# Early heads' one-hot tables of places made by GpSimd and ScalarE instead of VectorE

## What is computed

```
q = (hb @ w_q).reshape(C, PEER_HEADS, 2, PEER_DK_HALF)
s = jnp.einsum('thpd,hpnd->thpn', q, sub_keys).astype(jnp.float32)
sv, si = lax.top_k(s, PEER_TOPK)
cand = sv[:, :, 0, :, None] + sv[:, :, 1, None, :]
cidx = si[:, :, 0, :, None] * PEER_NKEYS + si[:, :, 1, None, :]
...
fv, fpos = lax.top_k(cand, PEER_TOPK)
eidx = jnp.take_along_axis(cidx, fpos, axis=-1).reshape(C, PEER_HEADS * PEER_TOPK)
g = jax.nn.softmax(fv, axis=-1).reshape(C, PEER_HEADS * PEER_TOPK)
```

## Time and profile before

| | us |
|---|---|
| median of 3 runs | 2003.02 |
| lowest, highest | 2001.21, 2003.94 |
| profiled execution, its own time | 2005.09 |
| its span | 2003.3 |
| TensorE busy | 1960.2 (98%) |
| VectorE, ScalarE, GpSimd busy | 1366.8, 792.7, 858.7 |
| mean granted TensorE clock of the span | 0.997 |

### The profile page before, as it was taken

One profiled execution on the slowest core, in us unless ns is written; L12 is line 12 of the kernel. 1 busy time (PEld: TensorE's weight loads), 2 busy tenths in 40 slices (PEclk: granted clock), 3 DMA queues, 4 the chain that ended last, 5 costly groups with the idle time before them and its releaser, 6 DMA issues.

```text
span 2003.3 us, 27875 instructions
## 1 busy us (share of the span) xinstructions
PE 1960.2 (98%) x9978; PEld 1440.4 (72%) x9978; DVE 1366.8 (68%) x3012; ACT 792.7 (40%) x1815; POOL 858.7 (43%) x680
## 2 busy tenths in 40 slices
PE   9999999999999999999999999999999999999998
PEld 8888876888768875788876666666666666666564
DVE  6742034333374566649999988888888888877767
ACT  3222233123563327621271575555556455410100
POOL 3544432428444753424424454443444434343343
PEclk9999999999999999999999999999999999999999
DMA  7655642515202411134489999999999999999999
GB/s 284 211 185 180 162 114 106 190 63 168 94 1 59 126 35 54 43 126 137 129 322 370 421 415 422 421 421 422 409 420 421 415 421 416 410 421 417 412 423 300
DMA packets 93644, 529.27 MB, mean 264 GB/s; under 512 B 10160, under 2 KB 14688, under 8 KB 44000
## 3 DMA queue, kind: packets, MB, share of 16 engines
q1 hardware_dynamic: 50112, 248.73, 33.5%
q0 software_dynamic: 37728, 270.55, 33.2%
q10 hardware_dynamic: 5696, 8.66, 2.1%
HBM read 520.56 MB, written 7.34 MB: 264 GB/s over the span
## 4 chain that ended last, share of the span: by engine, by line
DMA 26%; PE 22%; DVE 16%; POOL 4%; issue 2%; ACT 1%; another core or an unknown queue 0%; DVEq 0%; POOLq 0%; ACTq 0%
DMA work<-in_peer_uv,consts 14%; DMA ring<-in_peer_uv,consts 13%; PE ps L887 9%; PE ps L1325 3%; PE ps L1300 3%; DVE tables L2221 2%; POOL ring L2932 2%; DVE work L2196 1%; POOL work L2932 1%; DVE ring L2196 1%; PE ps L1192 1%; PE ps L937 1%; DVE work L1979 1%; DVE ring L2178 1%; DVE work L1972 1%
## 5 line engine op out<-in xcount | busy, mean ns | idle before, releaser
L1325 PE MATMUL ps<-work,tmp 128*128 128x512 f32 x1008 | 448.8, 598 | 16.0 <-DVE tmp L2255 15.9
L1300 PE MATMUL ps<-hT,work 128*128 128x256 f32 x1984 | 449.4, 381 | 0.0
L1300 PEld LDWEIGHTS ps<-hT,work 128*128 128x128 f32 x1984 | 373.3, 190 | 75.4 <-issue 29.7
L2832 POOL TENSOR_TENSOR w_lo<-ring,w_hi 128x1024 fp32r<-128x1024 f32 (+2 forms) x112 | 267.1, 2390 | 333.2 <-ACT w_hi L2337 314.6
L1325 PEld LDWEIGHTS ps<-work,tmp 128*128 128x128 f32 x1008 | 190.5, 191 | 240.4 <-issue 213.2
L2932 POOL DMA_INDIRECT ring<-in_peer_uv,consts x128 | 206.6, 1614 | 289.0 <-DVE tables L2221 255.2
L2932 POOL DMA_INDIRECT work<-in_peer_uv,consts x128 | 204.6, 1598 | 281.9 <-DVE tables L2221 224.7
L2337 ACT ACTIVATE w_hi<-ring 128x1024 fp32r<-128x1024 f32 (+2 forms) x116 | 120.4, 1041 | 359.9 <-PE ps L887 320.8
L2694 ACT ACTIVATE ring<-iota,consts 128x128 f16<-128x128 f32 x768 | 231.5, 426 | 0.0
L2196 DVE CUSTOM_DVE_ANT_0 ring<-ring,tables 128x1024 f32<-128x1024 f32 x128 | 155.7, 1222 | 70.6 <-DMA ring<-in_peer_uv,consts 68.4
L2747 ACT ACTIVATE hT<-hT 128x4 f32<-128x4 f32 (+1 forms) x66 | 13.6, 206 | 479.6 <-DVE hT L2196 479.5
(11 more groups left out here) (392 smaller groups left out, 3153.7 us busy)
## 6 DMA issues: line engine op xcount, KB each, us to landing
work<-in_peer_v SPq DMA_DIRECT2D x64, 1024.0 KB
work<-in_u_steps SPq DMA_DIRECT2D x62, 1024.0 KB
ring<-in_a_w_in SPq DMA_DIRECT2D x48, 512.0 KB, 4.3
ring<-in_ada_w SPq DMA_DIRECT2D x48, 512.0 KB, 5.0
ring<-in_peer_w_q SPq DMA_DIRECT2D x32, 512.0 KB, 3.5
ring<-in_a_w_out SPq DMA_DIRECT2D x16, 512.0 KB, 4.1
ring<-in_b_w_in SPq DMA_DIRECT2D x16, 512.0 KB, 4.3
ring<-in_c_in SPq DMA_DIRECT2D x12, 512.0 KB, 3.9
```

Source lines behind the costliest of these rows:

```text
L1300: mm = pe.matmul(ps[:, 4 + s, j * DT:(j + 1) * DT], u[s][:, j, k, :], hT[:, k, GATHERED * P:T], start=(k == 0), stop=(k == KD - 1))
L1325: mm = pe.matmul(ps[:, 2 * t + half, :], tmp[:, s, j * DT + t * P:j * DT + (t + 1) * P], v_ring[:, s, j, half * BANK:(half + 1) * BANK], s ...
L2832: pool.tensor_tensor(w_lo[q % NPIECE][:, 0:n], ring[:, at:at + n], w_hi[q % NPIECE][:, 0:n], ALU.subtract).then_inc(w_split, 1)
```

## The change

For heads 0 to 6 the two tables are made in three steps elsewhere. GpSimd, once `placed` tells it that `posf` is there, subtracts the counter from it (`place_off`). ScalarE squares the difference in place and then takes max(0, 1 - square) in place, so that 0 becomes 1 and every other whole number becomes 0 (`place_hot`). GpSimd waits for that and goes on as before. ScalarE does this in a function `hot_places`, which stands in its queue at seven fixed turns, `HOT_AT`: turns 0 to 16 are the early queries, turn 17 + f is late query f. So heads 0 to 4 are served right behind the copies of early queries 5, 8, 11, 13 and 15, heads 5 and 6 behind those of late queries 2 and 4. Head 7 stays with VectorE, with a new wait for the picks of head 5. To have semaphores for this, the four of the slabs of `x` become one, and ScalarE waits for all four slabs ahead of the first square. GpSimd also waits once for the load of `iota`.

```diff
+HOT_AT = (5, 8, 11, 13, 15, 19, 21)
...
-                for a in range(2):
-                    one_hot_place(step, r, NE, a, pick_eq[h % 2][a])
+                if h == PEER_H - 1:
+                    dve.wait_ge(picked, 2 * (h - 1))
+                    for a in range(2):
+                        one_hot_place(step, r, NE, a, pick_eq[h % 2][a])
...
+                    act.wait_ge(x_loaded, 16 * NT)
                     for t in range(NT):
-                        act.wait_ge(x_loaded[t], 16)
...
+            def hot_places(turn):
+
+                for h in range(PEER_H - 1):
+                    if HOT_AT[h] != turn:
+                        continue
+                    for a in range(2):
+                        eq = pick_eq[h % 2][a]
+                        act.wait_ge(place_off, 2 * h + a + 1)
+                        act.activation(eq, eq, ACT.Square).then_inc(place_hot, 1)
+                        act.wait_ge(place_hot, 4 * h + 2 * a + 1)
+                        act.activation(eq, eq, ACT.Relu, scale=-1.0, bias=1.0).then_inc(place_hot, 1)
+
             for f in range(2 * PEER_H + 1):
                 if f < 2 * PEER_H:
                     keep_query("pqT", "peer_s", f)
+                hot_places(f)
...
                     keep_late(f - 1)
+                hot_places(2 * PEER_H + 1 + f)
...
+            pool.wait_ge(row_loaded, 16 * 7)
             for h in range(PEER_H):
...
                 pool.wait_ge(placed, h + 1)
+                if h < PEER_H - 1:
+                    if h >= 2:
+                        pool.wait_ge(picked, 2 * (h - 1))
+                    for a in range(2):
+                        pool.tensor_tensor(pick_eq[h % 2][a],
+                                           early[h % 2].posf[:, a, :].unsqueeze(2).to_broadcast([P, EK, TOPK]),
+                                           iota[:, 0:TOPK].unsqueeze(1).to_broadcast([P, EK, TOPK]),
+                                           ALU.subtract).then_inc(place_off, 1)
                 for a in halves:
+                    if h < PEER_H - 1:
+                        pool.wait_ge(place_hot, 4 * h + 2 * a + 2)
```

More of the change, by code:

```diff
@@ L587, in network @@
         x_again = sem("x_again")
-        x_loaded = [sem(f"x_loaded{t}") for t in range(NT)]
+        x_loaded = sem("x_loaded")
         xT_loaded = [sem(f"xT_loaded{q}") for q in range(KD // 2)]
@@ L654, in network @@
         placed = sem("placed")
+        place_off = sem("place_off")
+        place_hot = sem("place_hot")
         pick_step = sem("pick_step")
@@ L764, in _ @@
                     for t in range(NT):
-                        sp.dma_start(a_x[:, t, :], ins["x"][t * P:(t + 1) * P, :]).then_inc(x_loaded[t], 16)
+                        sp.dma_start(a_x[:, t, :], ins["x"][t * P:(t + 1) * P, :]).then_inc(x_loaded, 16)
                     sp.dma_start(ident[:], ins["ident"]).then_inc(const_loaded, 16)
```

## The result

The changed kernel has a median of 2007.01 us (14 runs, 2004.59 to 2008.10) against 2003.71 us for the kernel before in the same comparison (14 runs). The ratio is 1.0015, 95% interval 1.0008 to 1.0022: some 3 us slower, 1.6 to 4.4. Two later comparisons gave 1.0009 (1.0000 to 1.0018) and 1.0013 (1.0004 to 1.0022). All three point the same way: it is slower. All three also lie within 0.2% in the middle, so it is the class that was forecast, no change beyond 0.2%; the size, 2.0 to 3.3 us between the medians, is larger than the forecast's 1.0.

What follows compares the result with a forecast made beforehand. TensorE and VectorE, both full, were taken to meet balanced at the tables `pairs`. 0 from VectorE and +0.8 us of TensorE's wait, +1.0 with larger activations half weighed, on 2003.02 gave 2004.0 us, range 2000.0 to 2009.0.

Steps and rivals of the forecast that it cites:

- the meeting point: At tables `pairs`, about 1000 us: TensorE and VectorE both full, VectorE at most about 0.1 us late; faster VectorE gains 0.
- the wait of TensorE: Near 961 us, for ScalarE's copy of late query 0 behind head 4's tables: 0.8 us, range 0.3 to 1.5.
- the forecast's own signs: Heads 2 to 4 waiting for GpSimd, head 7 near 986.5, VectorE idle 4 to 5 us, tables 1000.6 to 1001.8 us.
- A sign of being wrong: In VectorE's routing heads: above 11.3 us a head without a wait in them would speak for slower heads.
- the forecast's own 2001.2 to 2006.3: For the whole kernel: from no TensorE wait and no stall to a 1.5 us wait and the 1.8 us stall doubled.
- the slower rival: VectorE's heads lengthen with GpSimd busy beside them: 2007.1 us at 11.8 us a head, 2013 at 12.8; chance 0.13.
- a head's 10.26 us: VectorE's routing heads without two tables: 11.56 - 1.30, about 10.26 us each; 9.1 us gross gain over seven heads.
- second rival: VectorE's short instructions wait for GpSimd's, an estimated 2.4 us a head, a pace of 12.7 us; chance 0.13.
- threshold of 11.8 us: VectorE's head length giving TensorE waits of 2.4 us near 961 and 1.7 us at turn 21: +4.1 us, 2007.1.
- The rule of the Trainium skill: In VectorE's heads: two-SBUF-input instructions and GpSimd's SBUF reads exclude each other, conversions possibly too; line 1993 showed 0.1 us.
- The sum: Whole kernel: 0 from VectorE, +0.8 us from TensorE's wait, +1.0 us with larger activations half weighed; median 2004.0 us.
- the fourth rival: VectorE and ScalarE's unnamed 1.8 us stall at 1024.43 us can vanish or double: 1.8 us either way; no separate chance.

Runs made afterwards that it cites:

- experiment 5: Kernel before with one semaphore for the slabs of x, plus two more 128x512 GpSimd operations a head in heads 0 to 6; ratio 1.0029 (1.0018 to 1.0040).
- experiment 3: Kernel before without VectorE's tables of heads 0 to 6, GpSimd multiplying a zero in their place; ratio 1.0005 (0.9996 to 1.0015).
- the turns moved: Changed kernel with HOT_AT (5, 8, 11, 14, 17, 20, 23) instead of (5, 8, 11, 13, 15, 19, 21); ratios to the kernel before 1.0007 and 1.0001.
- experiment 2: Kernel before with only one semaphore and one wait for the four slabs of x; ratio 1.0002 (0.9993 to 1.0011).
- four activations: Kernel before with one semaphore for x; ScalarE waits for head 4's `placed` at turn 15 and makes four 128x512 activations; 2007.82 us, ratio 1.0008.
- six activations: Kernel before with one semaphore for x; ScalarE waits for head 4's `placed` at turn 15 and makes six 128x512 activations; ratio 1.0019 (1.0010 to 1.0028).
- experiment 4: Eleven late queries ahead of `pairs` instead of twelve: in the kernel without VectorE's tables of heads 0 to 6, ratio 1.0000; in the kernel before, 1.0030.

## Why the prediction was right, and where it was off

**What luck did.** The class came out as forecast, because the meeting point gives nothing back and the wait of TensorE is small. But most of the forecast's own signs did not come: heads 2 to 4 did not start on a wait for GpSimd, head 7 was placed at 991.08 and not near 986.5, VectorE did not idle 4 to 5 us, and the tables came at 1002.43, behind 1001.8. A sign of being wrong did come: heads of about 11.3 us and more without a wait in them. The 2007.01 us lie outside the forecast's own 2001.2 to 2006.3, in the part of the range that was there for the slower rival (the kernel before measured 0.7 us more this time than in the three runs). And it was luck that the contention took no more than the tables gave back: VectorE came to the tables 1.0 us early instead of 4.9, and experiment 5 shows what a late one costs.

**Right, and shown.** (a) The meeting point at `pairs` is balanced, and a faster VectorE is worth nothing there: experiment 3. (b) The change costs one wait of TensorE, for late query 0, because ScalarE stands at turn 15 for head 4: present in all three profiles, gone with the turns moved together with the 2.6 us. (c) An activation of 128x512 takes 0.61 to 0.63 us, against 0.6 taken. (d) The slabs of `x` cost nothing: experiment 2. (e) The first indirect transfer shows the shift: 2.12 us, as the tables (2.15).

**The step that failed: a head's 10.26 us.** I took VectorE's pace without the tables as 11.56 - 1.30 and let ScalarE's turns hold heads 2 to 4 by waits for the picks. Heads 0 to 6 came 11.0 to 12.3 us apart, 11.5 in the mean, and no head started on a wait for GpSimd. Experiment 3 shows 10.2 us where GpSimd has no more to do than before, so the subtraction was right for VectorE alone; experiment 5 shows what was missing, two operations of GpSimd for 0.7 us a head of VectorE, where the changed kernel lost 1.2. My second rival had the mechanism and about its size: it gave 11.3 us a head as the case where the sum still counts as no change, with a wait of 1.9 us near 961. A wait of 1.51 to 1.90 us came, and its threshold of 11.8 us wasn't reached. What the forecast had against it, that VectorE's heads stayed at 11.56 us with GpSimd beside them half the time, was a wrong reading: GpSimd's work lay beside the searches, which it doesn't slow. Only three short instructions grew, and the earlier trace rows had shown one of them at 276 instead of 195 ns.

The rule of the Trainium skill that the prediction named (SBUF — State Buffer, section "Who interferes with whom") fits these runs in kind: the adds with two inputs grew by up to 1.13 us (0.41 to 1.54) and the conversion by up to 1.1 (0.195 to 1.30), less than the 1.27 us of the operation of GpSimd beside them, and the searches not at all.

**From there the other sizes.** Head 7 was placed at 991.08 and not at 986.5, and VectorE idled 1.0 us ahead of `pairs` and 1.4 us ahead of the third table, not 4 to 5. Head 4 was placed 1.5 us later than forecast; the differences took 1.05 us each, not 1.27, so ScalarE began at 957.03 instead of 955.8. The block from there to the copy of late query 0 took 5.5 us, 0.3 less than forecast, so the copy was 0.9 us later than forecast and TensorE's scores behind it 1.7 us later than before (0.8 + 0.9), 1.51 us of that as a wait of its own; the scores behind the wait and turn 21 added 0.3 us. The sum with it would have been +2.0 us, a time of 2005.0; measured were 2.0 to 3.3 us, 0.4 of them outside the span.

**Left open: the 1.8 us of the earlier trace rows near 1024 us.** VectorE and ScalarE wait there, and each can only wait for one count of TensorE, `spread_summed`, which TensorE raises behind the 32 matmuls of a step (line 1291). In the kernel before the matmuls that VectorE's step needs end at 1024.10 us by their rows, and both engines go on at 1026.25, 2.1 us behind. In other profiles VectorE goes on 0.03 to 0.05 us behind such an end. First the kernel before, then the one with four activations, where the end is at 1025.87:

```profile
1026.25 0.42 DVE L2173 TENSOR_TENSOR ysum<-xres,consts 128x512 f16<-128x512 f16 x1 [1.82 <-remote]
```

```profile
1027.24 0.42 DVE L2174 TENSOR_TENSOR ysum<-xres,consts 128x512 f16<-128x512 f16 x1 [1.05 <-PE ps L1292]
```

Of the thirteen profiles, the five with all three tables at their old place have the full stall. In seven where a table has moved the count is not 2.1 us late: 1.2 and 1.4 in two (two more operations on GpSimd, four activations), and no idle time of that kind in the rest. But the thirteenth, the third profile of the changed kernel, has it in full with the tables moved. How much of a shift is left at the dense products goes with the stall. Tables 2.0 us late and no stall: 2.0 - 1.8 = 0.2, measured 0.3 to 0.4. Tables 1.8 late and 1.05 us of the stall left: 1.0, measured 1.0. Tables 4.8 late and no stall (six activations): 3.0, measured 3.3. Tables 2.4 late and nearly the whole stall: 2.3, measured 2.1. This is the fourth rival's 1.8 us, either way. Why the count comes late, no profile says; I didn't find an edit that would separate it.

**Left open: the way from there to the end.** The first two profiles of the changed kernel have the dense products only 0.3 to 0.4 us late, yet all three comparisons have it 2.0 to 3.3 us slower. The last dense product starts 1068.7, 1069.1 and 1069.8 us behind head 0 in the changed kernel, 1068.3 and 1068.0 with the turns moved; but the kernel before and its twin with one semaphore are themselves 1.2 us apart there (1066.4 and 1065.2). One profile a kernel can't trace the rest. The first indirect transfer is 1.7 us later against head 0 than with the turns moved (113.09 against 111.37); that the end hangs on it is argued and not shown. Nor does any run say what takes the 0.4 us outside the span. The kernels without VectorE's tables of heads 0 to 6 all have it (2.07 to 2.24 us between own time and span), and so far these are also the ones in which GpSimd waits for the load of `iota`.

## What to carry to other kernels

Before work is moved off a busy engine, look at what the engine's remaining instructions share with the one that gets the work: here two more GpSimd operations a head, with the old ones moved to a later place in it, took back 8.6 of the 9.1 us that VectorE was relieved of. Ask first where the busy engine next meets another, and whether it comes there early or late; if both come together, relief on one side is idle time, and a delay on either side has nothing there to hide in. And give an in-order engine a step that waits for a slower chain only behind the work that others need from it: one or two turns of 3.9 us later for four of the heads, the same edit cost nothing that the medians show.

## What the runs showed of the hardware that I had not expected

- An instruction of VectorE on 16 numbers a partition grew from 0.17 to 0.69 us, and one on 256 from 0.41 to 1.54 us, beside GpSimd's 1.05 to 1.27 us operations. With two more operations of GpSimd a head in each case, the three lines took 11.9, 15.7 and 16.4 us together: GpSimd's busy time alone doesn't give the cost, and which of the three grows depends on where in a head its operations fall.
- TensorE's granted clock stayed at 1.00 behind waits of 1.50, 1.51 and 1.90 us, and was 0.50 for about 3.5 us behind 2.81 us of standing, about as long behind 2.93 us (experiment 4) and for longer behind 4.30 us (the kernel with two more operations on GpSimd, 1007 to 1012 us):

```profile
1007.00:1008.00 1.00, 0.92 (x4) 0.83 (x5) 0.89 (x3) 0.00 (x0) 0.00 (x0) 0.50 1.01 426
1010.00:1012.00 2.00, 2.00 (x8) 1.73 (x8) 1.97 (x7) 0.39 (x1) 0.00 (x0) 0.50 1.01 426
```

- GpSimd's operations on 128x512 have two prices: 1.04 to 1.06 us for the subtraction of two broadcast operands, for a table times itself and for a broadcast zero times the key numbers, 1.27 us for a table times the key numbers.
- Two profiles can stand 3 us apart before the edit is reached, from a first load and from the granted clock; differences of 1 us are read from a fixed event on, not from the span.
